# Dividing the expert columns 72 to 56 and taking every second single-tile unit in rounded parts

## What is computed

```python
def blk(args):
    hx, e, gt = args
    act = jax.nn.gelu(jnp.einsum('nd,nhkd->nhk', hx, expert_u[e]), approximate=False)
    return jnp.einsum('nhk,nhkd->nd', gt * act, expert_v[e])
```

## Time and profile before

| | us |
|---|---|
| median of 3 runs | 3355.92 (3354.51 to 3357.80) |
| the profiled execution: time | 3360.74 |
| its span, first to last instruction | 3358.5 |
| `v` stage in it, first to last matmul | 1716.6 to 2295.4 |
| TensorE busy over the span | 99% |
| VectorE / ScalarE busy | 68% / 46% |

### The profile page before, as it was taken

How to read it: one execution, slowest core, us unless ns; L and a number is a source line. 1 busy time by engine, 2 the same in 40 slices (tenths; PEclk the granted TensorE clock), 3 DMA queues, 4 the chain that set the end, 5 groups by cost and what they waited for, 6 DMA issues and landing times. The chain is left out here.

```text
span 3358.5 us, 50459 instructions
## 1 busy us (share of the span) xinstructions
PE 3317.8 (99%) x20034; PEld 2744.7 (82%) x20034; DVE 2268.1 (68%) x2858; ACT 1542.6 (46%) x2405; POOL 732.4 (22%) x471
## 2 busy tenths in 40 slices
PE   8999999999999999999999999999999999999999
PEld 7877777778899999999986666667888877788887
DVE  4788666665487487488876676666788875565454
ACT  5564444343544576433432222225656544444863
POOL 0001000000189600388842121110122210000000
PEclk9999999999999999999999999999999999999999
DMA  6565434564556554588888888885433444455344
GB/s 244 191 204 171 158 125 152 168 240 180 201 196 204 200 203 152 199 279 274 276 310 314 322 315 315 322 304 208 165 141 142 151 172 176 169 200 188 133 156 163
DMA packets 148875, 704.00 MB, mean 210 GB/s; under 512 B 34156, under 2 KB 56460, under 8 KB 69946
## 3 DMA queue, kind: packets, MB, share of 16 engines
q1 hardware_dynamic: 121816, 622.99, 51.9%
q0 software_dynamic: 26864, 78.38, 7.2%
HBM read 743.29 MB, written 23.63 MB: 228 GB/s over the span
## 5 line engine op out<-in xcount | busy, mean ns | idle before, releaser
L241 DVE TENSOR_TENSOR lo_w<-ring,hi_w 128x1024 fp32r<-128x1024 f32 x372 | 455.5, 1224 | 514.9 <-ACT hi_w L235 499.3
L2127 PE MATMUL PS<-both_x,hi_w 128*128 128x256 f32 x4096 | 729.5, 281 | 2.8 <-POOL lo_w L243 2.8
L235 ACT CAST hi_w<-ring 128x1024 fp32r<-128x1024 f32 x412 | 431.2, 1047 | 585.2 <-DMA ring<-in_wstream 559.8
L2127 PEld LDWEIGHTS PS<-both_x,hi_w 128*128 128x128 f32 x4096 | 628.1, 189 | 3.2 <-ACT act_early L2391 3.1
L2127 PE MATMUL PS<-both_x,lo_w 128*128 128x256 f32 x2048 | 575.6, 281 | 0.0
L658 PE MATMUL PS<-hi_w,both_x 128*128 128x512 f32 (+2 forms) x1520 | 500.4, 399 | 5.1 <-DVE RKV L1670 3.1
L243 DVE TENSOR_TENSOR lo_w<-ring,hi_w 128x1024 fp32r<-128x1024 f32 x372 | 456.3, 1227 | 0.0
L236 ACT CAST hi_w<-ring 128x1024 fp32r<-128x1024 f32 x412 | 431.2, 1047 | 0.0
L2856 PE MATMUL PS<-hi_w,both_x 128*128 128x512 f32 x1232 | 401.5, 401 | 4.5 <-PEq L2028 1.8
L2127 PEld LDWEIGHTS PS<-both_x,lo_w 128*128 128x128 f32 x2048 | 384.5, 188 | 0.0
L658 PEld LDWEIGHTS PS<-hi_w,both_x 128*128 128x128 f32 x1520 | 285.3, 189 | 78.5 <-issue 12.3
(11 more groups left out here) (594 smaller groups left out, 5663.7 us busy)
## 6 DMA issues: line engine op xcount, KB each, us to landing
ring<-in_wstream SPq DMA_DIRECT2D x508, 1024.0 KB, 6.7
thin_w<-in_wstream SPq DMA_DIRECT2D x32, 1024.0 KB
act_dram<-act_early SPq DMA_DIRECT2D x38, 128.0 KB, 4.8
gates_dram<-gst POOLq DMA_DIRECT2D x8, 512.0 KB, 3.8
other_G<-staged SPq DMA_DIRECT2D x16, 256.0 KB, 2.3
R<-act_dram SPq DMA_DIRECT2D x64, 64.0 KB, 6.6
both_x<-other_G SPq DMA_DIRECT2D x1, 4096.0 KB, 19.2
act_dram<-act_late SPq DMA_DIRECT2D x26, 128.0 KB, 1.9
```

The costliest lines, as they stand in the source:

```text
L235: a.copy(hi_w[s][:, 0:HALF], ring[s][:, 0:HALF]).then_inc(S(f"hi{s}"), 1)
L241: v.tensor_tensor(lo_w[s][:, 0:HALF], ring[s][:, 0:HALF], hi_w[s][:, 0:HALF].bitcast(F32), ALU.subtract)
L2127: m = nc.tensor.matmul(PS[:, s, 0:T], wa[s][:, k * P:(k + 1) * P], xa[:, k, :], start=(k == 0 and p == 0), stop=(k == KC - 1 and p == 2))
```

## The change

The dividing line is moved: `HB = 72` thin units and `HA = 56` dense ones, in place of 64 and 64. `u_b` becomes 18 groups of four units and `u_a` 14; gathered rows now come from the first 72 x 128 experts. The table of gates keeps its 64 columns in DRAM (`TAB`), and the eight new columns are kept in `tab_c`, which takes the room that GG gives up. The order is DDDDDD, twelve times tD, then ttD and tD mixed, and again DtDtt... at the end.

From thin unit 12 on there is a third thin buffer (`third_w`, inside GG). From thin unit 27 on every odd one up to 69, 22 in all, is split as dense units are: ACT casts its gate and weights (`thin_high`), DVE makes the remainders (`thin_low`), and TensorE runs 12 products of the rounded type in place of 4 of float32 (`v_rounded`). There is one buffer `thin_hi` for all of them, so `thin_high(k)` waits until thin unit k-2 is finished.

```diff
-HK = PK // 2
-LEAD, CLOSE = 6, 2
+HB, HA, TAB = 72, 56, 64
+LEAD, CLOSE, TURNS = 6, 2, 12
...
-    freed_b = lambda k: at_a[3] if k < 2 else at_b[k - 2]
-    thin_w = (ring[3][:], over("thin_w", (P, UNIT), F32, hi_base + 3 * UNIT * 4)[:])
+    THREE, SPLIT0 = 12, 27
+    slot_b = lambda k: k % 2 if k < THREE else (k - THREE) % 3
+    freed_b = lambda k: at_a[3] if k < 2 else at_b[k - 2] if k < THREE + 2 else at_a[15] if k == THREE + 2 else at_b[k - 3]
...
+    rounded = [k for k in range(SPLIT0, HB - 2) if k % 2]
+    mul_tick = [at_b[k] - 3 - min(max(k - SPLIT0 + 4, 0), 3) for k in range(HB)]
...
+            def v_rounded(k):
+
+                r, wl = rounded.index(k), thin_lo[slot_b(k)]
+                t.wait_ge(S("thin_lo"), r + 1)
+                t.wait_ge(S("gate_lo"), r + 1)
+                for c in range(4):
+                    cs = slice(c * 512, (c + 1) * 512)
+                    nc.tensor.matmul(PS[:, c, :], gate_hi[:], thin_hi[:, cs], start=False, stop=False)
+                    nc.tensor.matmul(PS[:, c, :], gate_hi[:], wl[:, cs], start=False, stop=False)
+                    m = nc.tensor.matmul(PS[:, c, :], gate_lo[:], thin_hi[:, cs], start=False, stop=False)
                 m.then_inc(S("unit_used"), 1)
...
+            def thin_high(k):
+
+                b, w = slot_b(k), thin_w[slot_b(k)]
+                if k == SPLIT0:
+                    a.wait_ge(S("g_lo"), 26)
+                else:
+                    a.wait_ge(S("unit_used"), W0 + VB + at_b[k - 2] + 1)
+                a.wait_ge(S("gb_mul"), k + 1)
+                a.copy(gate_hi[:], act_b[:, k % AHEAD, :]).then_inc(S("gate_hi"), 1)
+                a.wait_ge(S(f"thin_in{b}"), 16 * turn_b[k])
+                a.copy(thin_hi[:, 0:HALF], w[:, 0:HALF]).then_inc(S("thin_hi"), 1)
+                a.copy(thin_hi[:, HALF:UNIT], w[:, HALF:UNIT]).then_inc(S("thin_hi"), 1)
...
-            for j in range(2, HK):
+            for j in range(2, HA):
                 high(j)
-                if j + 1 < HK:
+                if j + 1 < HA:
                     v_hi(j + 1)
+                for k in rounded:
+                    if j + 1 < HA and at_a[j + 1] < at_b[k] < (at_a[j + 2] if j + 2 < HA else VB):
+                        thin_high(k)
...
+            def thin_low(k):
+
+                r, w, wl = rounded.index(k), thin_w[slot_b(k)], thin_lo[slot_b(k)]
+                v.wait_ge(S("gate_hi"), r + 1)
+                v.tensor_tensor(gate_lo[:], act_b[:, k % AHEAD, :], gate_hi[:].bitcast(F32), ALU.subtract).then_inc(S("gate_lo"), 1)
+                v.wait_ge(S("thin_hi"), 2 * r + 1)
+                v.tensor_tensor(wl[:, 0:HALF], w[:, 0:HALF], thin_hi[:, 0:HALF].bitcast(F32), ALU.subtract)
...
-                for k in range(HK):
-                    if at_b[k] - 3 == p:
+                for k in range(HB):
+                    if mul_tick[k] == p:
                         times_b(k)
                         v.drain()
+                for k in rounded:
+                    if at_b[k] - 3 == p:
+                        thin_low(k)
```

More of the change, by code:

```diff
@@ L60 @@
 GROUPS = _g
-HK = PK // 2
-LEAD, CLOSE = 6, 2
+HB, HA, TAB = 72, 56, 64
+LEAD, CLOSE, TURNS = 6, 2, 12
 def v_sequence():
-    dense, sparse = list(range(HK)), list(range(HK))
+    dense, sparse = list(range(HA)), list(range(HB))
     seq = [(False, dense.pop(0)) for _ in range(LEAD)]
-    n, m = HK - CLOSE, 2 * HK - LEAD - CLOSE
+    for _ in range(TURNS):
+        seq += [(True, sparse.pop(0)), (False, dense.pop(0))]
+    n, m = len(sparse) - CLOSE, len(sparse) + len(dense) - CLOSE
     for i in range(m):
@@ L2006, in build @@
     adds_v = lambda p: [ADDS_U + i for i in range(ADDS_V) if add_at[i] == p]
-    add_tick = {s: i for i in range(HK) for s in adds_u(i)} | {s: HK + p for p in range(VB) for s in adds_v(p)}
+    add_tick = {s: i for i in range(HA) for s in adds_u(i)} | {s: HA + p for p in range(VB) for s in adds_v(p)}
     G0_FROM, X0_UNTIL = ADDS_U + 12, PK - 16
@@ L2067, in _ @@
                         .then_inc(S(f"act_out{s}"), 16)
-            for i in range(STEADY, HK):
+            for i in range(STEADY, HB):
                 refill_unit(i)
@@ L2143, in v_dense @@
             def v_dense(j):
-                s, h, first, last = slot_a(j), j % SLOTS, j == 0, j == HK - 1
+                s, h, first, last = slot_a(j), j % SLOTS, j == 0, j == HA - 1
                 t.wait_ge(S("v_lo"), j + 1)
@@ L2163, in v_thin @@
             def v_thin(k):
-                last = k == HK - 1
-                t.wait_ge(S(f"thin_in{k % 2}"), 16 * (k // 2) + 16)
+                last = k == HB - 1
+                t.wait_ge(S(f"thin_in{slot_b(k)}"), 16 * turn_b[k])
                 t.wait_ge(S("gb_mul"), k + 1)
                 for c in range(4):
-                    m = nc.tensor.matmul(PS[:, c, :], act_b[:, k % AHEAD, :], thin_w[k % 2][:, c * 512:(c + 1) * 512],
+                    m = nc.tensor.matmul(PS[:, c, :], act_b[:, k % AHEAD, :], thin_w[slot_b(k)][:, c * 512:(c + 1) * 512],
                                          start=False, stop=last)
@@ L2250, in _ @@
                         m.then_inc(S("route_ps"), 1)
-            with t.Fori(0, HK // SLOTS) as g:
+            with t.Fori(0, HA // SLOTS) as g:
                 for s in range(SLOTS):
@@ L2254, in _ @@
             for thin, k in V_SEQ:
-                if thin:
+                if thin and k in rounded:
+                    v_rounded(k)
+                elif thin:
                     v_thin(k)
@@ L2376, in _ @@
             scores_in(3)
-            for w in range(2 * HK):
+            for w in range(VB):
                 for j in at_unit(w):
@@ L2467, in _ @@
             for s in range(SLOTS):
-                g.wait_ge(S(f"act_out{s}"), 16 * (HK // SLOTS))
-            for i in range(CELL0, HK + VB):
+                g.wait_ge(S(f"act_out{s}"), 16 * (HB // SLOTS))
+            for i in range(CELL0, HA + VB):
                 if i <= ADD0:
-                    g.wait_ge(S("unit_used"), W0 + HK + i)
+                    g.wait_ge(S("unit_used"), W0 + HB + i)
                 for s in fetches(i):
@@ L2643, in _ @@
             places()
-            for i in range(ROUTED, HK):
+            for i in range(ROUTED, HB):
                 for j in at_unit(i):
@@ L2649, in _ @@
                 lo(i + SLOTS - 2)
-            for i in range(HK):
-                lo(HK + i + SLOTS - 2)
+            for i in range(HA):
+                lo(HB + i + SLOTS - 2)
                 if i:
@@ L2671, in _ @@
                     add_row(s)
-                for j in range(3, HK):
+                for j in range(3, HA):
                     if tick_a(j) == p:
```

94 lines of the change are left out of this document (54 added, 40 removed).

## The result

| | median of runs, us | range | profiled execution | its span | granted clock |
|---|---|---|---|---|---|
| before | 3357.8 | 3354.51 to 3359.35 | 3360.74 | 3358.5 | 0.998 |
| after | 3373.2 | 3369.14 to 3375.52 | 3375.52 | 3373.4 | 0.994 |

Five runs of each. The ratio after to before is 1.0045, with a 95% interval of 1.0034 to 1.0055: the change makes the kernel slower, by 15.4 us or 0.46%, where 2.9 us faster was forecast, and the time lies 4 us above the range.

What follows compares the result with a forecast made beforehand. PE alone was taken to bound the kernel, DVE and transfers next. The terms -16.9 - 14.7 + 19.8 + 0.9 + 2 + 5.6 + 0.4 gave -2.9 us, from 3355.9 to 3353 us, range 3341 to 3369.

Steps and rivals of the forecast that it cites:

- Parts 1 and 2: PE's work in v: eight units turned from dense to thin, -16.9 us, and 22 rounded units, -14.7; together 31.6 us shorter.
- Part 2: Rounded thin units in v: 12 matmuls in place of 24, 3.44 to 2.77 us for each of 22, -14.7 us.
- Part 3: Middle of v: ACT's order makes PE wait 3.3 us at six dense units, +19.8 us, bounds 0 to +23.
- Part 4: Landings of thin weights delay dense units in v: +0.9 us at the first rounded unit, +2 for the others.
- Part 5: DVE in v: needs 12.5 of 13.5 us, 92%, so it just holds; its lateness is put into the +2 for landings.
- Part 6: End of v: the first a_in unit's ring 0 is freed last, so all behind moves by +5.6 us; slow clock +0.4.
- The step that failed is the clock: First a_in unit: part of it may run at 1.2 GHz after PE idles, +0.4 us, within 0 and +2.8.
- The transfers: Later v: ten units need 366 GB/s without stalls, 339 with one; the sum stands while the six stalls are there.
- Rival A2: Later v: no stalls or late landings, but transfers bind at some 41.7 us for ten units; 3337 us, chance 0.03.
- A: Middle of v: the stalls from ACT's order and late landings don't come, -25 us, 3331 us; chance 0.11.
- B: v: landings past 8.6 us make each of 21 dense units wait for thin weights, +12 us, 3368 us; chance 0.24.

Runs made afterwards that it cites:

- Experiment 1: The kernel after, with ACT casting a dense unit's activations (hi_g) in front of the rounded thin unit's three casts; 3334.04 us, ratio 0.9929 to before.
- experiment 2: The kernel after with no thin unit rounded, the split of 72 and 56 and the third buffer kept; 3348.64 us, ratio 0.9973 to before.
- experiment 7: The kernel after with the 1 MB reload of the first tile of x issued seven units later; 3369.22 us, ratio 1.0037 to before.
- experiment 6: Experiment 1 with the three dense buffers' turn shifted at dense units 34 and 44, so ring 0 is free first; 3329.73 us, ratio 0.9917 to before.
- experiment 3: The kernel after, with PE running 12 products of a tile of zeros in front of the six dense units; 3363.56 us, ratio 1.0026 to before.
- experiment 4: The kernel after, with DVE at v's end adding the first tile's sums before making lo of the first a_in unit; 3369.11 us, ratio 1.0034 to before.
- (5): The kernel after with the changes of experiment 1 and experiment 4 together; 3332.57 us, ratio 0.9931 to before.

## Why the prediction was wrong

**Parts 1 and 2 were right.** Experiment 1 has the two gains with no wait in the way. Its v stage, from SP's first issue to the last, is 2262.53 - 1723.69 = 538.8 us, and before it was 2295.62 - 1722.41 = 573.2. Of the 34.4 us of difference, 1.4 are the old wait for lo_g and 1.2 shorter waits for weights, which leaves 31.8 for the forecast's 31.6. Part 2 alone measured 14.9 for 14.7 (experiment 2 against 1).

**Part 3 was right in place, cause and price.** Six waits stand at the six named units: 3.14, 4.11, 3.31, 3.14, 6.8 and 3.14 us. Experiment 1 shows that ACT's order is their cause. Four of them are 3.14 to 3.31 for the 3.3 forecast; the 4.11 and the 6.8 hold late landings besides, which belong to Part 4.

**Part 4 was a little small.** The wait at the first rounded unit, 0.9 forecast, didn't come. In its place 3.5 us came through one landing of 12.5 us (experiment 7), 0.9 in the wait of 4.11, whose casts began 0.87 us after the gate cast, and 3.1 in three short waits. Parts 3 and 4 together were 22.7 us and measured 26.7. The lo_g wait of 1.4 us in the kernel before is gone, so what was added is 25.3. The landings have a median of 7.3 us for the dense and 8.2 for the thin weights, against the earlier trace rows:

```profile
DMA to landing us min/median/max: 4.9/7.3/11.5
```

```profile
DMA to landing us min/median/max: 5.0/8.2/12.5
```

**Part 5 was right that DVE just holds.** PE waited for the rounded units' remainders for 0.4 us in all, and in experiment 1, with hi_g made early, for DVE not once before v's end. DVE's share in the later v there is 0.86 (266.20 of 310 us), a little under the 92% of the working.

**Part 6 was right.** +5.3 measured where 5.6 was forecast, and experiment 6 takes it back with the ring.

**The step that failed is the clock.** The sum had +0.4 for it, at the end of v alone, with bounds of 0 and 2.8. It read the page's row of full clock as a property of the stage, though Part 3 had just put six idle times of 3.3 us into it. The bounds came from the last 8.5 us of the span, 0.88, and were not applied to the middle. The runs show 9.5 us of it in v and 2.1 in a_in, and experiment 3 that the idle times cause it. By stages of the two traces (SP's first and last issue behind a unit of v, the first matmul of a_in and of the stage behind it):

| us | before | after | change | forecast |
|---|---|---|---|---|
| up to SP's first issue in v | 1722.4 | 1720.9 | -1.5 | 0 |
| v, first to last issue | 573.2 | 579.8 | +6.6 | -8.9 |
| to the first a_in matmul | 3.9 | 9.1 | +5.3 | +5.6 |
| a_in | 20.5 | 22.1 | +1.6 | +0.4 |
| all behind it | 1038.5 | 1041.5 | +3.0 | 0 |

The changes sum to +14.9, rounding apart, the forecasts to -2.9, and 17.8 us lie between them. The clock is the largest part: 9.5 in v and 1.2 in a_in (1.6 for 0.4), 10.7 in all. In v another 2.6 are waits for lo_g (25.3 added for 22.7), 0.2 waits for weights and 0.4 the wait for a rounded unit's remainder. The 2.8 us of v that are left are not placed; a part is the last matmul before each wait, which holds PE 0.17 us longer than it does in a run of matmuls, 1.5 us for nine waits by this estimate. The first and the last row lie within the scatter of the traces (see Open).

The Trainium skill, "TensorE: Matmul & The Clock Gate", HAM oscillation — how this bites in real kernels, describes just this: a gap in PE's work brings the clock back to its lower level, and the work behind the gap starts slow. The trace of the kernel after agrees, with 0.52 to 0.80 behind five gaps of 3.1 to 6.8 us, and differs behind one of 3.14 us, where the clock stayed at 1.00. The page's case should have been weighed beside Part 3.

**The transfers** were no bound. Experiment 1 needs 366 GB/s by the forecast's working, with no stall to give the queue rest. The queue's own view from 1950 to 2240 us of that kernel:

```profile
DMA packets 22839, 104.77 MB, mean 361 GB/s; under 512 B 5126, under 2 KB 10390, under 8 KB 10390
```

It moved 361 GB/s for 290 us, and PE waited for weights 0.4 us in all of v. The Trainium skill, "DMA: Bandwidth & Descriptors", Where 436 GB/s comes from, has about 358 GB/s for a core as what binds; here it didn't bind. Rival A2, built on it, is not borne out.

**The rivals.** A is what experiment 1 makes of the kernel: 3331 forecast, 3334 measured, with 3.0 us of slow clock at the start of v in it. B's 3368 lies near the 3373.2, but its mechanism is not what happened: three waits beyond Part 3's six and 3.1 us, not 21 waits with 14.7. The slower side came from a mechanism that no rival had.

**Open.** SP's first issue in v comes at 1720.5 to 1723.7 us in the eight kernels with the change, and at 1722.4 before. From the first matmul behind a_in to the end of the span it is 1038.5 us before and 1041.5 after, but in the other seven traces, with the same instructions there, it is 1038.3 to 1041.5. The value before is at the low end of this scatter and the value after at its high end, so neither difference can be put down to the change. Why the clock fell behind some waits of 3.1 us and not behind others, and why the wait of 6.8 us came in some kernels only, is open.

## What to carry to other kernels

When a cost model predicts idle times of PE of some 3 us, price the work behind each of them at the lower clock as well: here 23.7 us of such waits cost another 9.5. An operation that waits for a late event must not stand ahead of one that is needed sooner in the order of the same engine; moving one cast ahead of three others, on an engine that is 47% busy, was worth 39 us. Where a stall can't be removed, something harmless for PE to do in it keeps the clock up. And read the clock in windows behind every wait before you say that it didn't fall: the first matmul behind a wait may still be fast.

## What the runs showed of the hardware

The granted clock is not a function of the gap's length alone. The kernel after and experiments 4 and 7 have six waits of 3.13 to 6.84 us each in v. Behind 16 of these 18 the clock fell to the lower level, which cost 1.5 to 3.1 us each within the next 3 to 7 us. In two of the 16 the first us behind the wait was still at full clock. Behind the other two, both 3.14 us long and in front of the same dense unit (at 1994.99 in the kernel after, 1997.00 in experiment 7), it did not fall, though in experiment 4 it did at that unit, behind 3.13 us. This is the first of them, in the kernel after:

```profile
1980.00:2000.00 20.00, 16.86 (x67) 12.12 (x66) 15.05 (x17) 11.00 (x15) 3.42 (x3) 1.00 0.93 341
```

At the start of v, with PE busy without a break for over 10 us ahead, it fell behind idle times of 2.43 (experiment 6), 2.66 (1), 2.75 (5), 2.79 (7) and 3.13 us (3), and did not behind 1.56 (4), 2.15 (2), 2.90 (before) and 3.55 (after). Behind the gaps of 1.0 to 1.8 us in v it never fell in any of the nine traces. A stage mean of 0.97 hides all this, and the page's row of clocks by slices shows nines throughout; windows laid on the work behind each gap show it. Products of zeros in the gaps, 2.8 us of them, were enough to keep the clock up at all six places.
